# Reordering ScalarE's queue against the weight stream of a two-block fp32 transformer kernel, and reading two last blocks from PSUM

## The chip, the cores and the metric

One Trainium2 chip, one core of it. The metric is the device time of one execution in microseconds (us), as the median of several executions. All data are fp32, batch 1, 256 rows of 2048 channels.

## The reference, cut to what matters

The input `x` passes two blocks. The first has gMLP, dilated and compressed attention, a cross attention and a feed-forward layer of 8192 units. The second, in which nearly all of the change lies, is a gated linear attention over a context and a latent sequence, with an adaptive modulation by a condition, and a SwiGLU:

```python
def second_block(...):
    sh_m, sc_m, gt_m, sh_f, sc_f, gt_f = _modulation(c[:, None, :], w_ada, b_ada)
    csh_m, csc_m, ... = _modulation(c_ctx, w_ada, b_ada)
    h_lat = x * (1.0 + sc_m) + sh_m
    h_ctx = ctx * (1.0 + csc_m) + csh_m
    mix_lat, _ = _token_mixer(h_lat, h_ctx, ...)     # 4 heads, chunks of 64, two directions
    x = _layer_norm(ALPHA * x + gt_m * mix_lat, ln_mix_gain, ln_mix_bias)
    ffn_lat = _swiglu(x * (1.0 + sc_f) + sh_f, w_ffn_in, w_ffn_out)
    return _layer_norm(ALPHA * x + gt_f * ffn_lat, ln_ffn_gain, ln_ffn_bias)
```

`x` here is the first block's output, whose last steps are `x + square(relu(h @ w_up)) @ w_down` and a root mean square norm over the channels.

## The kernel before

**The weight stream.** The kernel is one stream of 974 half slots of weights. SyncE loads 1 MB (two halves, 128x1024 each) into a ring `RW`. For each half ScalarE (ACT) copies it rounded into a ring `RH` (L1161), VectorE (DVE) subtracts that from the weights into `RL` (L1947), and TensorE (PE) multiplies eight 128x128 tiles of both parts into PSUM (L489 the high part against high and low activations, 512 columns; L490 the low part against the high activations, 256 columns; L527 to L529 for products whose activations are the stationary side). `RH` and `RL` hold five halves: before ACT rounds half x it waits until PE has used half x - 4 (`a.wait_ge(s["used"], x - NR + 1)`, with NR = 5). A block is four halves for most products. At a block's end ACT copies the low sum from PSUM to the buffer `LT` (L1166), and DVE adds `LT` and then the high sum from PSUM to what the block is for (L2006, L2279 with L2281, L2825). The modulated input, like every input of a product, is a pair of buffers `AH` (rounded) and `AL` (the rest), drawn as `A` in the views.

**Lanes.** Every engine has its own queue, which it works off in order. The queues are written by generators, called lanes here: `run(a, b, ...)` lets each lane write one step, in the order of its arguments, and again until all are at their end. One such round is a tick; in most of them one half is multiplied. Inside one tick the argument order decides which lane's instructions come first in an engine's queue, and it was one order for all engines. `schedule()` calls the same lanes for each engine. `after(n, lane)` starts a lane n ticks late, `idle(n)` is a lane of n empty ticks, `chain` sets lanes one behind another, `both` side by side.

**The places the change touches**, in the order of the program:

- *last_down with modulate_ctx*: the last column blocks of `w_down`, and beside them the modulation of the context. For a pair of channel tiles DVE scales (L2436), ACT rounds the result into `AH` (L1556), DVE makes the rest `AL` (L2426).
- *scale_x with k2*: the sum of squares of the norm. DVE adds up squares (L2028), PE sums over partitions (L582, L583), ACT makes the reciprocal root (L1235, L1241). The first halves of `w_k` (`k2`) are beside it.
- *context heads*: four heads (`ctx_head`), each with a decay (PE L909), transposes of the weighted keys (PE L950, which need DVE L2562) and the states (PE L929), beside `v2` and `k2`.
- *q2 with modulate_lat*: the modulation of the latent rows, the same lines as above, beside the product with `w_q`.
- *latent heads*: `lat_head(h)` beside `v2` and `bg2`. A direction's queries `Q4` (DVE L2636) are needed by PE L1017. `bg2` makes the merge gates: at each of its blocks' ends DVE adds the sum up in `GB` (L2006), and ACT stores `GB` by a DMA (L1764, to `gate`), for which it waits for DVE.
- *out2*: the block output's product; its evaluation is `gated` (L2825), then the mean and the squares of the layer norm.
- *fin with modulated_ffn*: the first halves of `w_ffn_in`, whose input is modulated in eight pairs of channel tiles: DVE removes the mean (L2834) and scales (L2885), ACT rounds (L1887), DVE makes the rest (L2882); then `x` itself is scaled (DVE L2891, ACT L1894). PE needs pair p at an eighth of the first block pair's halves, in order.
- *fout part 2*: the last product, with `gated` and the final layer norm behind it (ACT's lanes in all this are at L1549, L1655, L1878).

Of the kernel before, what the change touches and what calls it, by code (L numbers as in the profile page):

```python
# [15 lines left out]
S = 256  # L16
# [144 lines left out]
class Lanes:  # L161
    pass
# [986 lines left out]
def scalar_program(nc, m, io):  # L1149
    a, s, l = nc.scalar, m.s, m.l  # L1150
    num, banks, later = Numbers(), Banks(m), Later()
    L = Lanes()

# [9 lines left out]
    def low_part(g):  # L1163

        a.wait_ge(s["used"], num.half)
        a.activation(pair2(m.LT[g % 2]), m.sum_l[g % 2], ACT.Copy).then_inc(s["lt"], 1)  # L1166

    def gemm(blocks, halves, evac, zipped=False):
        rest, g0 = None, num.block
        num.block += blocks  # L1170
        for b, c in steps(blocks, halves, zipped):
            prepare(num.half)
            num.half += 1
            if rest is not None:
                next(rest, None)
            yield
            if c == halves - 1:
                if rest is not None:
                    exhaust(rest)
                low_part(g0 + b)  # L1180
                if num.factor is not None:
                    next(num.factor, None)
                rest = evac(b, g0 + b)
                next(rest, None)
                if b % 2 == 1 and b + 1 < blocks:
                    yield
        exhaust(rest)
        yield
# [570 lines left out]
    def bg2():  # L1759
        def evac(b, g):  # L1760
            n, i = divmod(num.kept, 2)
            num.kept += 1
            a.wait_ge(m.pair[g % 2], g // 2 + 1)
            a.dma_start(io["gate"][n][:, i * 512:i * 512 + 512], m.GB).then_inc(l["kept"], 16)  # L1764
            yield
        yield from gemm(4, 4, evac)
# [106 lines left out]
    def out2():  # L1873
        a.preload_act_table_set("natural_log_exp_and_others")
        yield from gemm(8, 4, normed(0))
        num.last_of_a = num.half
# [39 lines left out]
    def fout(part, first, n):  # L1916
        if part == 2:
            a.preload_act_table_set("natural_log_exp_and_others")
        yield from gemm(8, n // 4, normed(1) if part == 2 else nothing)
        num.fouts.append(num.half)  # L1920
# [15 lines left out]
def vector_program(nc, m, io):  # L1936
# [13 lines left out]
    def gemm(blocks, halves, evac, zipped=False):  # L1950
        rest, g0 = None, num.block
        num.block += blocks
        for b, c in steps(blocks, halves, zipped):
# [5 lines left out]
            if c == halves - 1:  # L1959
                num.lt += 1  # L1960
# [809 lines left out]
    def gated_x(N, which, mods):  # L2770
# [10 lines left out]
        def evac(b, g):  # L2781
# [4 lines left out]
            gated(which, b, g)  # L2786
# [28 lines left out]
    def gated(which, p, g):  # L2815

        v.wait_ge(s["lt"], num.lt)
# [3 lines left out]
        for low in (True, False):  # L2821
            for i in range(2):
                x = m.X[:, (2 * p + i) * S:(2 * p + i + 1) * S]
                part = m.LT[g % 2][:, i * S:i * S + S] if low else m.sum_h[g % 2][:, i, :]
                r = v.scalar_tensor_tensor(x, part, m.mod(which, 2 * p + i), x, ALU.mult, ALU.add)  # L2825
# [25 lines left out]
    L.out2 = lambda: gemm(8, 4, gated_x(0, 2, 20))  # L2851
# [61 lines left out]
    def fout(part, first, n):  # L2913
# [3 lines left out]
        yield from gemm(8, n // 4, evac)  # L2917
# [241 lines left out]
def schedule(L):  # L3159
# [34 lines left out]
    for h in range(4):  # L3194
        run(slow(L.lat_head(h), 1.0 if h == 3 else 1.42), chain(idle() if h == 3 else L.v2(), L.bg2()))
# [10 lines left out]
    run(chain(L.fin(0, 8), L.fin(8, 4), L.fout(0, 0, 16), L.fin(12, 4), L.fin(16, 4), L.fout(1, 16, 16),  # L3206
              L.fin(20, 2), L.fout(2, 32, 12)), modulated, after(10, L.ada((5,), (2.2,))))
# [153 lines left out]
```

## Time and profile before

| | |
|---|---|
| time, 3 runs | 3120.05 us median (3114.98 to 3121.35) |
| the profiled execution's own time | 3117.38 us, its span 3116.0 us |
| PE / DVE / ACT busy | 3004.7 / 2178.2 / 1464.0 us (96%, 70%, 47%) |
| mean granted clock of PE | 0.983 of 2.4 GHz |

The profile is of one execution. "Busy" is time in which an engine works on an instruction; what an engine waited for is inferred from the semaphore that came last. The granted clock is 1.00 at 2.4 GHz and 0.50 at 1.2 GHz.

### The profile page before, as it was taken

Reading aid. Unit: us, or ns where it says so; the run is one execution under the profiler, and the core shown is the slowest. Engines: PE = TensorE matmul, PEld = TensorE weight load, DVE = VectorE, ACT = ScalarE, POOL = GpSimd, SP = SyncE. Lnnn points to the kernel's source line nnn. Section 1 sums busy time; section 2 is a strip of 40 time slices with the busy share of each in tenths; the row PEclk is TensorE's granted clock in tenths of the full one; section 3 lists DMA queues with packets and bytes.
Section 4 is the critical chain, followed back from the end, with each engine's and each line's share of the span. In section 5 each row is a group of like instructions: output and inputs, shape, how many; then the busy total and the mean of one; then the engine's idle time right before and its main releaser. Section 6 shows DMA issues by size and latency. Waiting matters only on the chain.

```text
span 3116.0 us, 40256 instructions
## 1 busy us (share of the span) xinstructions
PE 3004.7 (96%) x16588; PEld 2559.7 (82%) x16588; DVE 2178.2 (70%) x2686; ACT 1464.0 (47%) x1955; POOL 8.5 (0%) x21
## 2 busy tenths in 40 slices
PE   8999898999999999999999999999998999999998
PEld 7887787888888888777787777888877888888886
DVE  6455866899899886677766666648886775555557
ACT  5434654544444444445444443544545444444444
POOL 0000000000000000000000000000000000000000
PEclk9989998999999999999999999999999999999999
DMA  6535233677767785456654444558644775555552
GB/s 257 193 143 180 105 137 122 224 262 259 259 251 267 288 310 203 162 210 246 233 209 163 179 170 173 215 216 330 222 177 182 284 263 185 185 185 189 189 188 109
DMA packets 106661, 648.60 MB, mean 208 GB/s; under 512 B 11856, under 2 KB 11856, under 8 KB 42352
## 3 DMA queue, kind: packets, MB, share of 16 engines
q1 hardware_dynamic: 99936, 621.86, 54.5%
q10 hardware_dynamic: 4608, 16.78, 1.4%
q0 software_dynamic: 1936, 7.41, 0.7%
q8 instruction: 131, 2.15, 0.3%
q14 instruction: 50, 0.41, 0.0%
HBM read 635.52 MB, written 10.49 MB: 207 GB/s over the span
## 4 chain that ended last, share of the span: by engine, by line
PE 78%; DVE 14%; ACT 4%; issue 3%; DMA 0%; SPq 0%; ACTq 0%; DVEq 0%
PE PS L489 41%; PE PS L490 21%; DVE RL L1947 5%; PE PS L527 3%; PE PS L529 3%; PE PS L528 3%; DVE G L2358 2%; ACT RH L1161 2%; PE PS L1017 1%; PE PS L727 1%; PE PS L929 1%; DVE G L2006 1%; ACT G L1362 1%; DVE X L2279 0%; DMA RW<-in_w_ckv 0%
## 5 line engine op out<-in xcount | busy, mean ns | idle before, releaser
L489 PE MATMUL PS<-A,RH 128*128 128x512 f32 x4544 | 1634.5, 404 | 42.1 <-DVE RL L1947 14.9
L1947 DVE TENSOR_TENSOR RL<-RW,RH 128x1024 fp32r<-128x1024 f32 x974 | 1178.3, 1222 | 606.5 <-ACT RH L1161 601.3
L1161 ACT ACTIVATE RH<-RW 128x1024 fp32r<-128x1024 f32 x974 | 1014.0, 1054 | 732.3 <-PE PS L490 585.0
L490 PE MATMUL PS<-A,RL 128*128 128x256 f32 x4544 | 1281.6, 282 | 0.0
L489 PEld LDWEIGHTS PS<-A,RH 128*128 128x128 f32 x4544 | 864.7, 190 | 260.1 <-issue 36.3
L490 PEld LDWEIGHTS PS<-A,RL 128*128 128x128 f32 x4544 | 869.1, 191 | 3.2 <-issue 2.6
L489 PE MATMUL PS<-H,RH 128*128 128x512 f32 x2304 | 816.4, 396 | 5.0 <-DVE RL L1947 5.0
L490 PE MATMUL PS<-H,RL 128*128 128x256 f32 x2304 | 652.0, 283 | 0.0
L489 PEld LDWEIGHTS PS<-H,RH 128*128 128x128 f32 x2304 | 433.4, 188 | 107.2 <-issue 4.0
L490 PEld LDWEIGHTS PS<-H,RL 128*128 128x128 f32 x2304 | 433.9, 188 | 0.4
L1166 ACT ACTIVATE LT<-PS 128x512 f32<-128x512 f32 x234 | 139.2, 595 | 354.9 <-PE PS L490 354.5
L2358 DVE SCALAR_TENSOR_TENSOR G<-G,SILT 128x1024 f32<-128x1024 f32 x210 | 263.5, 1278 | 8.4 <-DMA G<-in_w_ada 8.4
L527 PE MATMUL PS<-RH,A 128*128 128x512 f32 x416 | 166.5, 400 | 0.1
L529 PE MATMUL PS<-RL,A 128*128 128x512 f32 x416 | 162.8, 391 | 0.0
L528 PE MATMUL PS<-RH,A 128*128 128x512 f32 x416 | 162.7, 391 | 0.0
L2006 DVE TENSOR_TENSOR G<-PS,LT 128x512 f32<-128x512 f32 x116 | 79.7, 687 | 87.0 <-ACT LT L1166 80.9
L527 PEld LDWEIGHTS PS<-RH,A 128*128 128x128 f32 x416 | 78.5, 189 | 19.8 <-issue 3.2
L528 PEld LDWEIGHTS PS<-RH,A 128*128 128x128 f32 x416 | 78.4, 189 | 17.1 <-issue 1.4
L529 PEld LDWEIGHTS PS<-RL,A 128*128 128x128 f32 x416 | 78.5, 189 | 16.7
L1525 ACT ACTIVATE G<-G 128x512 f32<-128x512 f32 x32 | 20.2, 632 | 130.8 <-DVE G L2391 130.8
L1362 ACT ACTIVATE G<-G,SM 128x256 f32<-128x256 f32 (+1 forms) x56 | 24.8, 444 | 67.3 <-DVE SM L2175 67.3
L2825 DVE SCALAR_TENSOR_TENSOR X<-LT,MODT,X 128x256 f32<-128x256 f32 x64 | 28.2, 482 | 38.6 <-ACT LT L1166 38.2
(253 smaller groups left out, 1606.9 us busy)
## 6 DMA issues: line engine op xcount, KB each, us to landing
RW<-in_w_fin SPq DMA_DIRECT2D x88, 1024.0 KB, 4.8
G<-in_w_ada SPq DMA_DIRECT2D x160, 512.0 KB, 5.9
RW<-in_w_up SPq DMA_DIRECT2D x64, 1024.0 KB, 5.0
RW<-in_w_down SPq DMA_DIRECT2D x64, 1024.0 KB, 5.0
RW<-in_w_fout SPq DMA_DIRECT2D x44, 1024.0 KB, 4.8
RW<-in_w_v SPq DMA_DIRECT2D x32, 1024.0 KB, 4.8
RW<-in_w_bg SPq DMA_DIRECT2D x32, 1024.0 KB, 5.0
RW<-in_w_k SPq DMA_DIRECT2D x16, 1024.0 KB, 4.8
```

The costliest lines, as they stand in the source:

```text
L489: t.matmul(bank[:, :], wh[:, k, cols], x, start=first and k == 0, stop=False, skip_group_check=True)
L490: done = t.matmul(bank[:, 0:256], wl[:, k, cols], x[:, 0, :], start=False, stop=last and k == 3, skip_group_check=True)
L527: t.matmul(out, xh, wh[:, k, :], start=first and k == 0, stop=False, skip_group_check=True)
L528: t.matmul(out, xl, wh[:, k, :], start=False, stop=False, skip_group_check=True)
L529: done = t.matmul(out, xh, wl[:, k, :], start=False, stop=last and k == 1, skip_group_check=True)
L727: done = t.matmul(bk.ap[:, i * 128:i * 128 + 128], v, pt[0:n, j * 128:j * 128 + 128], start=x == 0, stop=x == len(ops) - 1)
L1161: a.activation(m.high(x), m.slot(j)[:, x % 2 * HC:x % 2 * HC + HC], ACT.Copy).then_inc(s["hi"], 1)
L1166: a.activation(pair2(m.LT[g % 2]), m.sum_l[g % 2], ACT.Copy).then_inc(s["lt"], 1)
L1362: x = a.activation(sc[:, i * n:i * n + n], src[:, i * n:i * n + n], ACT.Exp, bias=sm[:, i:i + 1], scale=scale, accum_out=sm[:, 2 + i:3 + i])
L1947: v.tensor_tensor(m.low(x), m.slot(j)[:, x % 2 * HC:x % 2 * HC + HC], m.high(x).bitcast(F32), ALU.subtract).then_inc(s["lo"], 1)
L2006: v.tensor_tensor(pair2(out), m.sum_h[g % 2], pair2(m.LT[g % 2]), ALU.add).then_inc(m.pair[g % 2], 1)
L2358: v.scalar_tensor_tensor(acc, m.ada_slot[cb][at], silu, acc, ALU.mult, ALU.add).then_inc(s["av"], 1)
```

## The change

On ACT alone (`weights_first`), the products' lane comes before the lane beside it in each tick, in six places; on DVE, PE and SyncE the lane comes first. In last_down and in fin the products came first on every engine before, so what changes there is DVE's order (and nothing in ACT's). The sum of squares (`scale_x`) begins two ticks later. The idle tick between context heads 1 and 2 stands ahead of head 0 instead. The latent modulation takes one step ahead of the first tick. ACT's stores of the gate come two ticks later. And in the last block of `out2` and of the last `fout`, DVE reads the low sum from PSUM itself and ACT's copy is gone (`direct`). No instruction of SyncE or GpSimd moves.

```diff
 class Lanes:
+    weights_first = False
+    def beside(self, lane, products):
+        return (products, lane) if self.weights_first else (lane, products)
...
+    L.weights_first = True          # in ScalarE's lanes only
...
-    def low_part(g):
+    def low_part(g, last=False):
+        if last:
+            return
         a.wait_ge(s["used"], num.half)
         a.activation(pair2(m.LT[g % 2]), m.sum_l[g % 2], ACT.Copy).then_inc(s["lt"], 1)
...
-                low_part(g0 + b)
+                low_part(g0 + b, direct and b == blocks - 1)
...
+        if late:
+            yield
+            exhaust(rest)
+            return
         exhaust(rest)
         yield
...
             num.kept += 1
+            yield
+            yield
             a.wait_ge(m.pair[g % 2], g // 2 + 1)
             a.dma_start(io["gate"][n][:, i * 512:i * 512 + 512], m.GB).then_inc(l["kept"], 16)
             yield
-        yield from gemm(4, 4, evac)
+        yield from gemm(4, 4, evac, late=True)
...
-    def gated(which, p, g):
-
-        v.wait_ge(s["lt"], num.lt)
+    def gated(which, p, g, direct=False):
+
+        if direct:
+            v.wait_ge(s["used"], num.half)
+        else:
+            v.wait_ge(s["lt"], num.lt)
...
-                part = m.LT[g % 2][:, i * S:i * S + S] if low else m.sum_h[g % 2][:, i, :]
+                part = m.sum_h[g % 2][:, i, :]
+                if low:
+                    part = m.sum_l[g % 2][:, i, :] if direct else m.LT[g % 2][:, i * S:i * S + S]
...
-    run(L.last_down(), after(6, L.modulate_ctx()))
-    run(L.scale_x(), L.k2(0, 0, 2))
+    run(*L.beside(after(6, L.modulate_ctx()), L.last_down()))
+    run(*L.beside(after(2, L.scale_x()), L.k2(0, 0, 2)))
     L.low_rank(0)
     beside = L.ada((4,), (2.25,))
-    run(chain(L.ctx_head(0), L.ctx_head(1), idle(1), L.ctx_head(2), L.ctx_head(3)),
-        chain(L.v2(), L.v2(), L.k2(0, 2, 2), L.v2(), L.v2()), beside=beside)
-    run(L.modulate_lat(), L.last_states(), L.q2(), beside=beside)
+    heads = chain(idle(1), L.ctx_head(0), L.ctx_head(1), L.ctx_head(2), L.ctx_head(3))
+    run(*L.beside(heads, chain(L.v2(), L.v2(), L.k2(0, 2, 2), L.v2(), L.v2())), beside=beside)
+    modulated = L.modulate_lat()
+    next(modulated)
+    run(*L.beside(both(modulated, L.last_states()), L.q2()), beside=beside)
...
-        run(slow(L.lat_head(h), 1.0 if h == 3 else 1.42), chain(idle() if h == 3 else L.v2(), L.bg2()))
+        run(*L.beside(slow(L.lat_head(h), 1.0 if h == 3 else 1.42), chain(idle() if h == 3 else L.v2(), L.bg2())))
...
-    run(chain(L.fin(0, 8), L.fin(8, 4), L.fout(0, 0, 16), L.fin(12, 4), L.fin(16, 4), L.fout(1, 16, 16),
-              L.fin(20, 2), L.fout(2, 32, 12)), modulated, after(10, L.ada((5,), (2.2,))))
+    products = chain(L.fin(0, 8), L.fin(8, 4), L.fout(0, 0, 16), L.fin(12, 4), L.fin(16, 4), L.fout(1, 16, 16),
+                     L.fin(20, 2), L.fout(2, 32, 12))
+    run(*L.beside(modulated, products), after(10, L.ada((5,), (2.2,))))
```

The changed file has more lines ahead of these places, so its numbers are higher: L1161 becomes L1169 (rounding), L1166 L1176, L1947 L1963, L2834 L2855, L2885 L2906, L2882 L2903, L489 and L490 L496 and L497, L582 and L583 L589 and L590.

**DVE's queue at the start of fin.** L1947 is the subtraction of one half of weights, L2834, L2885 and L2882 are the modulation. Before:

```order
1612 L2882 SCALAR_TENSOR_TENSOR A<-G,SM,A 128x256 x2
1613 L1947 TENSOR_TENSOR RL<-RW,RH 128x1024
1614 L2834 TENSOR_TENSOR X<-X,RS 128x512
1615 L2885 SCALAR_TENSOR_TENSOR G<-X,SM,RS 128x256 x2
1616 L2882 SCALAR_TENSOR_TENSOR A<-G,SM,A 128x256 x2
1617 L1947 TENSOR_TENSOR RL<-RW,RH 128x1024
```

The same place of the changed kernel:

```order
1602 L2903 SCALAR_TENSOR_TENSOR A<-G,SM,A 128x256 x2
1603 L2855 TENSOR_TENSOR X<-X,RS 128x512
1604 L2906 SCALAR_TENSOR_TENSOR G<-X,SM,RS 128x256 x2
1605 L2903 SCALAR_TENSOR_TENSOR A<-G,SM,A 128x256 x2
1606 L1963 TENSOR_TENSOR RL<-RW,RH 128x1024
1607 L2855 TENSOR_TENSOR X<-X,RS 128x512
```

In each tick the modulation now stands ahead of the subtraction; ACT's queue there is as it was.

**PE's queue at the sum of squares** (L582 and L583, behind the last half of `w_down`, whose input is `H`, and around the first halves of `w_k`, whose input is `A`). Before:

```order
6449 L489 MATMUL PS<-H,RH 128x512
6450 L490 MATMUL PS<-H,RL 128x256
6451 L582 MATMUL PS<-G,C 128x256
6452 L583 MATMUL PS<-G,C 128x256
6453 L489 MATMUL PS<-A,RH 128x512
```

The same two matmuls in the changed kernel:

```order
6481 L496 MATMUL PS<-A,RH 128x512
6482 L497 MATMUL PS<-A,RL 128x256
6483 L589 MATMUL PS<-G,C 128x256
6484 L590 MATMUL PS<-G,C 128x256
6485 L496 MATMUL PS<-A,RH 128x512
```

They stand 32 matmuls, which is two halves, further back.

**ACT's queue in latent head 3**, around a store of the gate (L1764, now L1780) and the roundings beside it. Before:

```order
783 L1617 ACTIVATE G<-G 128x512
784 L1161 ACTIVATE RH<-RW 128x1024
785 L1166 ACTIVATE LT<-PS 128x512
786 L1764 DMA gate<-G 128x512
787 L1161 ACTIVATE RH<-RW 128x1024 x3
```

In the changed kernel:

```order
793 L1631 ACTIVATE G<-G 128x512
794 L1176 ACTIVATE LT<-PS 128x512
795 L1169 ACTIVATE RH<-RW 128x1024 x2
796 L1780 DMA gate<-G 128x512
797 L1169 ACTIVATE RH<-RW 128x1024 x2
```

Two roundings now stand between the copy and the store.

## Rows read from the trace of the kernel before

**Rows 1.** The page: busy time of each engine, and the chain that ended last

```profile
PE 3004.7 (96%) x16588; PEld 2559.7 (82%) x16588; DVE 2178.2 (70%) x2686; ACT 1464.0 (47%) x1955; POOL 8.5 (0%) x21
...
PE 78%; DVE 14%; ACT 4%; issue 3%; DMA 0%; SPq 0%; ACTq 0%; DVEq 0%
```

**Rows 2.** PE's waits over the span: waited for, us, times, longest

```profile
PE PS L489 <- DVE RL L1947: 19.9, 15, 10.9
PE PS L489 <- DVE A L2882: 12.1, 5, 4.5
...
PE PS L489 <- DVE A L2426: 4.8, 3, 2.3
...
PE PS L582 <- DVE G L2028: 4.3, 2, 3.6
PE PS L950 <- DVE G L2562: 3.5, 2, 2.8
...
PE PS L909 <- DVE ALR L2462: 2.1, 2, 1.1
...
PE PS L1017 <- DVE G L2636: 1.4, 1, 1.4
```

**Rows 3.** Windows: stretch, length, busy of PE, PEld, DVE, ACT, POOL; PEclk, DMA share, GB/s

```profile
1224.47:1246.95 22.48, 22.48 (x130) 19.70 (x129) 15.61 (x26) 10.31 (x14) 0.00 (x0) 1.00 0.55 196
1246.95:1264.43 17.48, 15.03 (x82) 12.23 (x81) 14.03 (x20) 10.13 (x13) 0.00 (x0) 1.00 0.50 180
1303.76:1315.64 11.88, 8.27 (x38) 6.89 (x37) 5.28 (x7) 4.12 (x6) 0.00 (x0) 0.86 0.37 142
1362.20:1377.21 15.01, 12.18 (x53) 9.14 (x51) 11.94 (x18) 5.17 (x7) 0.00 (x0) 0.89 0.48 187
1500.69:1519.90 19.21, 14.38 (x66) 11.59 (x65) 14.20 (x20) 6.34 (x9) 0.00 (x0) 0.82 0.47 177
2334.78:2339.34 4.56, 4.56 (x16) 3.90 (x17) 3.39 (x6) 1.85 (x3) 0.00 (x0) 0.59 0.00 0
2339.34:2365.42 26.08, 18.45 (x82) 14.89 (x81) 18.56 (x33) 10.19 (x17) 0.00 (x0) 0.81 0.23 81
2365.42:2397.74 32.32, 29.14 (x161) 24.57 (x161) 17.64 (x27) 19.12 (x30) 0.00 (x0) 0.99 0.66 240
2403.36:2442.19 38.83, 38.83 (x226) 33.97 (x225) 31.42 (x31) 19.19 (x22) 0.00 (x0) 1.00 0.76 281
```

**Rows 4.** DVE's timeline in fin: start, us, line, tile, idle before and releaser

```profile
2342.21 1.23 DVE L1947 TENSOR_TENSOR RL<-RW,RH 128x1024 fp32r<-128x1024 f32 x1 [1.14 <-ACT RH L1161]
2343.35 0.68 DVE L2834 TENSOR_TENSOR X<-X,RS 128x512 f32<-128x512 f32 x1
2344.14 0.88 DVE L2885 SCALAR_TENSOR_TENSOR G<-X,SM,RS 128x256 f32<-128x256 f32 x2
2344.94 0.87 DVE L2882 SCALAR_TENSOR_TENSOR A<-G,SM,A 128x256 fp32r<-128x256 f32 x2
```

**Rows 5.** ACT's timeline in fin, same columns

```profile
2345.06 0.91 ACT L1887 ACTIVATE A<-G,SM 128x256 fp32r<-128x256 f32 x2 [2.88 <-DVE G L2885]
2345.87 1.04 ACT L1161 ACTIVATE RH<-RW 128x1024 fp32r<-128x1024 f32 x1
```

**Rows 6.** ACT's timeline in latent head 3

```profile
1895.80 2.01 ACT L1161 ACTIVATE RH<-RW 128x1024 fp32r<-128x1024 f32 x2 [4.51 <-DVE G L2006]
```

**Rows 7.** Timeline of DVE and PE in latent head 0, second direction

```profile
1679.19 0.69 DVE L2636 TENSOR_TENSOR G<-G,SM 128x512 f32<-128x512 f32 x1
...
1679.93 0.70 PE L1017 MATMUL PS<-G 128*128 128x512 f32 x1
```

**Rows 8.** ACT's timeline behind the last weight product

```profile
3096.98 0.60 ACT L1166 ACTIVATE LT<-PS 128x512 f32<-128x512 f32 x1 [4.55 <-PE PS L490]
```

**Rows 9.** One line's instructions: duration in ns, min/median/max

```profile
L2825 DVE SCALAR_TENSOR_TENSOR X<-LT,MODT,X x64: 475/480/489, 2240.2 to 3098.0; 128x256 f32<-128x256 f32 x64
L2825 DVE SCALAR_TENSOR_TENSOR X<-PS,MODT,X x64: 473/480/486, 2241.1 to 3098.9; 128x256 f32<-128x256 f32 x64
```

More of the change, by code:

```diff
@@ L161 @@
 class Lanes:
-    pass
+    weights_first = False
+    def beside(self, lane, products):
+        return (products, lane) if self.weights_first else (lane, products)
 class Later:
@@ L1161, in prepare, with gemm @@
             a.activation(m.high(x), m.slot(j)[:, x % 2 * HC:x % 2 * HC + HC], ACT.Copy).then_inc(s["hi"], 1)
-    def low_part(g):
+    def low_part(g, last=False):
+        if last:
+            return
         a.wait_ge(s["used"], num.half)
         a.activation(pair2(m.LT[g % 2]), m.sum_l[g % 2], ACT.Copy).then_inc(s["lt"], 1)
-    def gemm(blocks, halves, evac, zipped=False):
+    def gemm(blocks, halves, evac, zipped=False, direct=False, late=False):
         rest, g0 = None, num.block
@@ L1874, in out2 @@
         a.preload_act_table_set("natural_log_exp_and_others")
-        yield from gemm(8, 4, normed(0))
+        yield from gemm(8, 4, normed(0), direct=True)
         num.last_of_a = num.half
@@ L1918, in fout @@
             a.preload_act_table_set("natural_log_exp_and_others")
-        yield from gemm(8, n // 4, normed(1) if part == 2 else nothing)
+        yield from gemm(8, n // 4, normed(1) if part == 2 else nothing, direct=part == 2)
         num.fouts.append(num.half)
@@ L1948, in prepare, with gemm @@
                             ALU.subtract).then_inc(s["lo"], 1)
-    def gemm(blocks, halves, evac, zipped=False):
+    def gemm(blocks, halves, evac, zipped=False, direct=False):
         rest, g0 = None, num.block
@@ L1959, in gemm @@
             if c == halves - 1:
-                num.lt += 1
+                num.lt += not (direct and b == blocks - 1)
                 if rest is not None:
@@ L2785, in evac @@
                     v.wait_ge(s["xa"], 4)
-            gated(which, b, g)
+            gated(which, b, g, b == 7)
             evacuated(g)
@@ L2849, in finish @@
         v.wait_ge(s["nrs_a"], 3 * N + 3)
-    L.out2 = lambda: gemm(8, 4, gated_x(0, 2, 20))
+    L.out2 = lambda: gemm(8, 4, gated_x(0, 2, 20), direct=True)
     def gains():
@@ L2916, in fout @@
         evac = gated_x(1, 5, 32) if part == 2 else gated_part
-        yield from gemm(8, n // 4, evac)
+        yield from gemm(8, n // 4, evac, direct=part == 2)
     def gated_part(b, g):
```

## The prediction, made before the changed kernel ran

> **What bounds the kernel now.** I read the page first: PE is busy 3004.7 of 3116.0 us, and the chain that ended last runs through PE for 78%, DVE 14% and ACT 4% [rows 1]. The change removes no matmul, so it can only fill PE's pauses. PE's waits, grouped by what ended them, say which pauses those are: for `RL`, for the modulated pairs (L2882, L2426), for the sum of squares (L2028), for keys of a context head (L2562) and for `Q4` (L2636), 46 us in all with waits that this change doesn't reach (the start of the kernel alone holds 10.9 of `RL`'s 19.9) [rows 2]. The waits leave out what a pause does to the clock, so I priced places by windows that begin and end with a half of weights: an undisturbed half takes 22.48/8 = 2.81 us in `down` and 38.83/14 = 2.77 us in `fin`, both at clock 1.00, while stretches with long pauses show 0.81 to 0.86 and the first half of fin 0.59, which is 4.56 us for 2.77 us of work [rows 3].
>
> **The ring of waits.** In fin a tick takes 4.74 us in a steady pattern. DVE sat idle 1.14 us before its subtraction, waiting for ACT's rounding, and ACT sat idle 2.88 us before its L1887, waiting for DVE's L2885 [rows 4, 5]. DVE can't start the modulation of a tick before that tick's subtraction; ACT can't round before it has done L1887 of the pair before. So neither works ahead, though there are free slots in the ring. With the modulation first on DVE, L2885 no longer stands behind the subtraction that waits for ACT, and the ring is open.
>
> **Part by part**, against the profiled time of 3117.4 us.
>
> *last_down, with the modulation of the context.* Five halves take 17.48 us where 5 x 2.81 = 14.05 are work [rows 3]. The pattern is the one of the ring, with L2436 and L1556. Nothing else limits the stretch: DVE is busy 14.03 of 17.48 us and 15.61 of 22.48 ahead of it. **-3.4**; with the modulation first, the subtraction is late by 2.2 us at most (0.73 + 1.48 us for its pieces at their largest), and the ring holds five halves.
>
> *Sum of squares.* Two halves take 11.88 us, 6.26 above 5.62 [rows 3]. PE's wait is 3.6 us of it [rows 2], the rest the two matmuls of the sum and a slow clock of 0.86. After, PE has two halves (5.5 us) to do first, so L2028 is there in time; the matmuls themselves stay, about 0.5. **-5.8**. Behind it, ACT makes the reciprocal root later by two halves; the scaled `x` isn't read before the latent modulation (`alpha_x` follows q2), which hides it.
>
> *Context heads.* Head 0 starts one tick later. The decay's wait of 1.1 us (L909) goes. The transposes' wait of 2.8 us [rows 2], in a stretch of 15.01 us at clock 0.89 with DVE busy 11.94 [rows 3], goes only in small part: DVE reaches L2562 through work of its own, which moves back by the same tick. With 0.7 us for the smaller wait at head 1 (3.5 less 2.8) **-1.8**, between 0 and -4.5 (all of these waits).
>
> *q2 with the modulation of the latent rows.* Four halves take 19.21 us, 7.97 above 4 x 2.81, at clock 0.82 [rows 3]; 4.8 are PE's waits for L2426 [rows 2]. Here DVE already had the modulation first, and the ring is ACT's: its L1556 waits for DVE, and its rounding stands behind that. One step ahead brings every pair forward by a tick (19.21/4 = 4.8 us), and three ticks lose DVE's idle of 1.1 us before the subtraction, taken from fin's pattern [rows 4]: 8.1 us in all, against 7.97 by which PE would want the last pair earlier. That is just enough: **-7.9**, down to -4 if one pair is late and the clock falls once.
>
> *Latent heads.* Head 3 alone has a wait, 1.4 us for L2636 [rows 2]. ACT stood 4.51 us before its rounding because the store of the gate waits for DVE's L2006 [rows 6], and the subtraction ahead of L2636 waited for that rounding. With the store two ticks later the rounding is early. **-1.4**, by the wait itself, without a slow stretch behind it. A store that lands late could hold DVE's next sum in `GB`: sums are four halves (11.2 us) apart, and two ticks of them (5.6 us) now pass before the store starts. The rows don't show how long it may take; I take no loss, and 1 us for each of the 16 blocks of `bg2` in a rival.
>
> *Last blocks from PSUM.* ACT's copy of 0.60 us goes, at the end of the kernel [rows 8] and at the end of out2, where PE has no weights to multiply meanwhile: **-1.2**. L2825 itself takes 480 ns from `LT` and 480 ns from PSUM [rows 9], so nothing is lost. The Trainium skill's page "VectorE: DVE Perf Modes", in the section "The TRN2 errata — SBUF-src ops pay a fixed extra latency per instruction", has a source in PSUM cost more fixed cycles (120 against 58) than one in SBUF, some 65 ns per instruction at its clock. By it, two reads at each end would give back 0.26 us in all, and the part would bring 0.9. The two rows of this trace do not show the difference, in 64 instructions each (where one operand, `X`, is in SBUF either way).
>
> *fin.* From the first half to the last late one are 4.56 + 26.08 + 32.32 us for 16 halves, which need 16 x 2.77 = 44.4: 18.6 above [rows 3]. The first 1.8 (slow clock behind the layer norm's tail) stay. In the middle 26.08 - 5 x 2.77 = 12.2: after the change a tick of DVE is its own work, from the starts of the rows 1.14 + 0.79 + 0.80 and 0.87 for L2882, 3.6 us in place of 4.74 [rows 4]. The L2882 shown is pair 3's and ends at 2345.8; two idles and one subtraction ahead of it go, 1.14 us each, so it ends at 2342.4, and the next pairs 3.6 us apart: 2346.0, 2349.6, 2353.2. PE multiplies two pairs in a half, but repeats them for the second block before it takes 4: from 2339.34 on it wants pair 3 after 1.5 halves (2343.5), 4 after 3 (2347.7), 5 after 3.5 (2349.0) and 6 half a half later, after its wait for 5 (2351.0). So PE still waits 0.6 and 2.2 us, with one slow half (1.8, as in fin's first) behind. 12.2 - 4.6 is 7.6, and pair 7's early coming (its step is a short one) adds 0.4: 8.0 go. In the last part 32.32 - 27.7 = 4.6 is the ring with L1894 and L2891 in it; 4.0 go. **-12.0**, between -8 and -14.
>
> The sum is 3.4 + 5.8 + 1.8 + 7.9 + 1.4 + 1.2 + 12.0 = **33.5 us**, so 3083.9 for the profiled execution. Its 3117.4 stand 2.7 below the median of the three runs; the median of the changed kernel then is 3120.05 - 33.5 = 3086.55, **3086.5**.
>
> **The rivals.**
>
> *A. As summed*, 3077 to 3096: **0.72**. For it speaks that every term is a stretch with pauses in one place, whose cause is an order that is gone. Its bounds are 0 and -4.5 in the context, -4 in q2, -8 and -14 in fin: between -33.5 + 1.8 + 3.9 + 4.0 = -23.8 (3096.3) and -33.5 - 2.7 - 2.0 = -38.2 (3081.9); the lowest run of before lies 5.1 under its median, and with that the lower end is 3077.
>
> *B. DVE is the limit where the ring was.* In the window of q2 it is busy 14.20 of 19.21 us, in fin's 18.56 of 26.08 [rows 3]; the subtractions that ACT now offers earlier fill its gaps ahead of the modulation. If the pairs come half as early as placed, fin and q2 give 10 instead of 20: **3096.5**, chance **0.14**. Against it: the changed queue puts the modulation first on DVE.
>
> *C. The rounding first costs the heads.* ACT does what it has for a head one rounding (1.04 us [rows 5]) later, and at eight directions and four context heads PE wants the result just when it is there: L2636 ended at 1679.88, PE's L1017 began at 1679.93 [rows 7], and heads 1 and 2 look the same. If each of the 12 is late by 1.04 us, 12.5 us go back, **3099**, chance **0.07**. Against it: rounding first lets DVE's subtraction, which stands in the same queue ahead of the head's pieces, start at once, which is 1 us to the good.
>
> *D, the slower side: a whole tick is lost per head.* If ACT's rounding in its turn waits for PE (the ring is full, slot x - 4 in use), the head's piece behind it waits up to 2.8 us more, and the clock falls as in fin's first half, 1.8. Then 12 x 4.6 = 55 go back against the 33.5: 3120.05 - 33.5 + 55 = **3141.5**; with 7.3 of the 12 places late it is even with before. ACT is busy 47% [rows 1] and mostly waits for PE at its roundings, which speaks for it; the steps of a head that have an idle tick ahead speak against. Chance **0.04**.
>
> *E. The change doesn't do what it says:* pauses reappear as waits for a landing DMA or another semaphore (16 us at the gate stores, the rest where a pair or a key is late again), within 6 us of before, 3114 to 3126: **0.03**.
>
> **How the numbers follow.** About 0.2% (6 us) is what a measurement of this kernel can tell from no change. A, B and C are faster by more, 0.93; D gives slower 0.04; E gives same 0.03. The range is to hold 8 in 10: A's from 3077 on, and it takes in the times of B (3096.5) and C (3099), up to 3100; what is left out is D, E and the tails.
>
> **What would show it.** The granted clock near 1.00 where it was 0.86 and 0.82 (sum of squares, q2). PE's waits for L2028 (but the 0.7 that lie elsewhere) and L2426 gone; those for L2882 down from 12.1 us to some 7, 4.5 of which are the start. DVE's waits for the rounding gone from fin's first twelve halves, and DVE's ticks there 3.6 us. ACT's idle of 4.51 before a rounding gone. The span's end some 0.6 us nearer to the last L490. It is wrong if PE shows new waits of over 1 us at L1017, L950 or L994 (C, D), if DVE's subtraction is late at L489 in places that were quiet, or if DVE waits at L2006 for a store of the gate.

## The result

The changed kernel takes **3080.6 us** (median of 4 runs, 3074.7 to 3082.5) against 3117.5 us of the kernel before beside it (3113.5 to 3121.4): a ratio of 0.9878, 95% interval 0.9858 to 0.9898. Repeated later with five runs it was 3078.2 against 3119.2, 0.9874 (0.9855 to 0.9892). 3086.5 was predicted, 3077 to 3100 as the range. In the profiled executions the span fell from 3116.0 to 3079.4 us, by 36.6; the prediction's sum was 33.5.

The page of the changed kernel, busy time by engine and the chain that ended last:

```profile
PE 2993.7 (97%) x16588; PEld 2553.5 (83%) x16588; DVE 2178.0 (71%) x2686; ACT 1461.0 (47%) x1953; POOL 8.5 (0%) x21
...
PE 85%; DVE 10%; ACT 3%; issue 2%; DMA 1%; SPq 0%; ACTq 0%; DVEq 0%
```

The work is the same (ACT has the two copies less), DVE's share of the chain went from 14% to 10% [rows 1]. PE's waits in the changed kernel:

```profile
PE PS L496 <- DVE RL L1963: 12.5, 4, 11.0
...
PE PS L496 <- DVE A L2903: 6.7, 3, 4.5
...
PE PS L957 <- DVE G L2578: 3.0, 1, 3.0
...
PE PS L916 <- DVE ALR L2478: 1.1, 1, 1.1
...
PE PS L496 <- DVE A L2442: 0.5, 1, 0.5
```

Against [rows 2], `RL` went from 19.9 to 12.5 us (11.0 of it the first load), the pairs of fin from 12.1 to 6.7 (4.5 of it the start), those of q2 from 4.8 to 0.5; the wait for `Q4` and the 3.6 us for the sum of squares are gone. What stands is the context's head 0, 3.0 us. The windows that answer to [rows 3], with the same halves in them (last_down, the sum of squares, the two halves behind it, head 0, q2, then three of fin and fin undisturbed):

```profile
1247.73:1261.77 14.04, 14.04 (x82) 12.30 (x81) 11.86 (x14) 7.56 (x10) 0.00 (x0) 1.00 0.49 177
1301.09:1306.71 5.62, 5.62 (x34) 4.90 (x33) 2.60 (x3) 2.10 (x3) 0.00 (x0) 1.00 0.48 182
1306.71:1313.18 6.47, 6.47 (x38) 5.66 (x37) 4.44 (x5) 3.92 (x6) 0.00 (x0) 1.00 0.50 203
1352.98:1366.97 13.99, 11.01 (x46) 8.64 (x45) 13.42 (x24) 5.18 (x8) 0.00 (x0) 0.88 0.52 201
1491.71:1502.81 11.10, 11.10 (x66) 9.71 (x65) 9.15 (x12) 5.92 (x7) 0.00 (x0) 1.00 0.78 291
2308.98:2313.23 4.25, 4.16 (x16) 3.63 (x17) 4.14 (x10) 2.76 (x5) 0.00 (x0) 0.64 0.00 0
2313.23:2330.02 16.79, 14.61 (x82) 12.22 (x81) 16.19 (x30) 8.82 (x14) 0.00 (x0) 1.00 0.35 126
2330.02:2358.29 28.27, 28.27 (x162) 24.52 (x161) 22.29 (x32) 21.10 (x33) 0.00 (x0) 1.00 0.70 258
2363.94:2403.52 39.58, 39.58 (x226) 34.34 (x225) 28.80 (x28) 17.89 (x20) 0.00 (x0) 1.00 0.75 279
```

last_down takes 14.04 us in place of 17.48, all of it matmuls. The sum of squares took 11.88 and with the next two halves 17.4; now it is 5.62 + 6.47 = 12.1. q2's four halves take 11.10 in place of 19.21. fin's middle takes 16.79 in place of 26.08, its last part 28.27 in place of 32.32.

In fin, DVE's and ACT's timeline of the changed kernel (start, length, line):

```profile
2316.44 1.22 DVE L1963 TENSOR_TENSOR RL<-RW,RH 128x1024 fp32r<-128x1024 f32 x1
2317.58 0.68 DVE L2855 TENSOR_TENSOR X<-X,RS 128x512 f32<-128x512 f32 x1
2318.37 0.88 DVE L2906 SCALAR_TENSOR_TENSOR G<-X,SM,RS 128x256 f32<-128x256 f32 x2
2319.16 0.87 DVE L2903 SCALAR_TENSOR_TENSOR A<-G,SM,A 128x256 fp32r<-128x256 f32 x2
2319.96 1.22 DVE L1963 TENSOR_TENSOR RL<-RW,RH 128x1024 fp32r<-128x1024 f32 x1
```

```profile
2319.28 0.91 ACT L1903 ACTIVATE A<-G,SM 128x256 fp32r<-128x256 f32 x2 [1.65 <-DVE G L2906]
```

DVE's rows stand one behind another without an idle bracket: a tick is 2319.96 - 2316.44 = 3.52 us where it was 4.74 [rows 4], and ACT's idle time before L1903 fell from 2.88 to 1.65 [rows 5]. That DVE is now what sets the pace there is seen from the missing brackets.

### The profile page after: what moved, and what is told of

Its sections match the earlier page's. It is cut to its first block, busy times and chain, and to the rows that moved or that the text cites. A ratio compares the mean times of both kernels' runs of the same rounds, so it can differ in the third digit from the quotient of the medians.

```text
span 3079.4 us, 40253 instructions
## 1 busy us (share of the span) xinstructions
PE 2993.7 (97%) x16588; PEld 2553.5 (83%) x16588; DVE 2178.0 (71%) x2686; ACT 1461.0 (47%) x1953; POOL 8.5 (0%) x21
## 4 chain that ended last, share of the span: by engine, by line
PE 85%; DVE 10%; ACT 3%; issue 2%; DMA 1%; SPq 0%; ACTq 0%; DVEq 0%
PE PS L496 46%; PE PS L497 23%; DVE RL L1963 3%; PE PS L534 3%; PE PS L536 3%; PE PS L535 3%; DVE G L2374 1%; ACT RH L1169 1%; PE PS L734 1%; PE PS L1024 1%; PE PS L936 1%; ACT G L1376 1%; PE PS L870 0%; PE PS L916 0%; DMA RW<-in_w_ckv 0%
## 5 line engine op out<-in xcount | busy, mean ns | idle before, releaser
L496 PE MATMUL PS<-A,RH 128*128 128x512 f32 x4544 | 1629.5, 403 | 28.5 <-DVE RL L1963 11.2
L1963 DVE TENSOR_TENSOR RL<-RW,RH 128x1024 fp32r<-128x1024 f32 x974 | 1178.4, 1222 | 559.3 <-ACT RH L1169 553.0
L1169 ACT ACTIVATE RH<-RW 128x1024 fp32r<-128x1024 f32 x974 | 1015.9, 1054 | 780.9 <-PE PS L497 634.9
L497 PE MATMUL PS<-A,RL 128*128 128x256 f32 x4544 | 1279.4, 282 | 0.0
L496 PEld LDWEIGHTS PS<-A,RH 128*128 128x128 f32 x4544 | 861.7, 190 | 245.5 <-issue 31.6
L497 PEld LDWEIGHTS PS<-A,RL 128*128 128x128 f32 x4544 | 865.6, 190 | 3.1 <-issue 2.6
L496 PE MATMUL PS<-H,RH 128*128 128x512 f32 x2304 | 814.0, 395 | 1.3 <-DVE RL L1963 1.3
L497 PE MATMUL PS<-H,RL 128*128 128x256 f32 x2304 | 651.4, 283 | 0.0
L496 PEld LDWEIGHTS PS<-H,RH 128*128 128x128 f32 x2304 | 432.8, 188 | 101.3 <-issue 1.2
L497 PEld LDWEIGHTS PS<-H,RL 128*128 128x128 f32 x2304 | 433.2, 188 | 0.4
L1176 ACT ACTIVATE LT<-PS 128x512 f32<-128x512 f32 x232 | 138.3, 596 | 346.3 <-PE PS L497 345.9
L734 PE MATMUL PS<-G 128*128 128x128 f32 (+1 forms) x184 | 35.8, 342 | 20.4 <-ACT G L1388 20.4
```

The costliest lines, as they stand in the source:

```text
L496: t.matmul(bank[:, :], wh[:, k, cols], x, start=first and k == 0, stop=False, skip_group_check=True)
L497: done = t.matmul(bank[:, 0:256], wl[:, k, cols], x[:, 0, :], start=False, stop=last and k == 3, skip_group_check=True)
L734: done = t.matmul(bk.ap[:, i * 128:i * 128 + 128], v, pt[0:n, j * 128:j * 128 + 128], start=x == 0, stop=x == len(ops) - 1)
L1169: a.activation(m.high(x), m.slot(j)[:, x % 2 * HC:x % 2 * HC + HC], ACT.Copy).then_inc(s["hi"], 1)
L1963: v.tensor_tensor(m.low(x), m.slot(j)[:, x % 2 * HC:x % 2 * HC + HC], m.high(x).bitcast(F32), ALU.subtract).then_inc(s["lo"], 1)
```

## The experiments

Each is the changed kernel with one or a few edits. Since the places lie far apart, each edit was read in its own window, which is far sharper than the whole time: the halves between the places take the same time from run to run, but for what the last section tells of.

**1. DVE's order of before** in last_down and fin; the other queues untouched.

```diff
-    run(*L.beside(after(6, L.modulate_ctx()), L.last_down()))
+    run(L.last_down(), after(6, L.modulate_ctx()))
...
-    run(*L.beside(modulated, products), after(10, L.ada((5,), (2.2,))))
+    run(products, modulated, after(10, L.ada((5,), (2.2,))))
```

> The changed kernel with VectorE's order of before in last_down and in fin (the subtraction ahead of the modulation); the queues of ScalarE, TensorE and SyncE are those of the changed kernel. Theory of the ring (each of the two engines waits for the other once per tick): the five halves 382 to 386 take 17.5 us again instead of 14.05, the 16 halves 710 to 725 take 62 to 63 us instead of 49.3, a tick of DVE in fin 4.7 us; together 17 us slower, some 3097.5. Rival, that these stretches gained by something else (VectorE's share of work, the clock after the layer norm's tail): under 5 us of it come back.

Measured: 3097.4 us (ratio to before 0.9942, 0.9926 to 0.9959). Windows of last_down and of fin's second and third part:

```profile
1247.78:1265.27 17.49, 15.04 (x82) 12.25 (x81) 14.05 (x21) 10.13 (x13) 0.00 (x0) 1.00 0.49 174
2318.46:2342.99 24.53, 16.62 (x80) 13.54 (x80) 18.30 (x33) 10.20 (x17) 0.00 (x0) 0.92 0.25 86
2342.99:2375.26 32.27, 29.14 (x164) 24.68 (x162) 17.27 (x26) 18.73 (x30) 0.00 (x0) 1.00 0.66 235
```

17.49 us again, and 24.53 + 32.27 = 56.8 against 45.1: 3.4 and 11.7 us come back. A tick of DVE in fin is 4.74 us again (its subtractions start at 2330.47 and 2335.21). This one swap on one engine gives back 15.1 of the 36.6 us by which the span fell.

**2. The same order on both engines**, the lane ahead of the products, in last_down and fin. DVE keeps the new order, ACT gets the other.

```diff
-    run(*L.beside(after(6, L.modulate_ctx()), L.last_down()))
+    run(after(6, L.modulate_ctx()), L.last_down())
...
-    run(*L.beside(modulated, products), after(10, L.ada((5,), (2.2,))))
+    run(modulated, products, after(10, L.ada((5,), (2.2,))))
```

> The changed kernel with the lane ahead of the products on ScalarE too, in last_down and fin: VectorE has the new order and ScalarE the one that it had in q2 before. Theory: what opens the ring is that the two engines have opposite orders; with the same order on both the ring is closed again whichever it is: a tick of fin takes 4.8 us, the 16 halves 710 to 725 some 62 us, last_down's five 17 us: +16 us, 3097. Rival: VectorE's order alone was the fault: the time stays at 3081.

Measured: 3096.5 us, one run. DVE's timeline in fin, and the windows of last_down (halves 381 to 385, which are the late ones here) and of fin's second part:

```profile
2324.63 1.23 DVE L1963 TENSOR_TENSOR RL<-RW,RH 128x1024 fp32r<-128x1024 f32 x1 [1.14 <-ACT RH L1169]
...
2329.37 1.23 DVE L1963 TENSOR_TENSOR RL<-RW,RH 128x1024 fp32r<-128x1024 f32 x1 [1.13 <-ACT RH L1169]
```

```profile
1244.92:1261.80 16.88, 14.77 (x82) 12.25 (x81) 13.13 (x20) 9.27 (x13) 0.00 (x0) 1.00 0.47 173
2319.63:2341.70 22.07, 16.54 (x81) 13.69 (x80) 16.90 (x29) 8.86 (x16) 0.00 (x0) 0.83 0.26 96
```

A tick of fin is 4.74 us, to the hundredth that of the kernel before, with the same idle 1.14 us. In last_down DVE's idle before the subtraction is back too, 1.05 us in each of two ticks. So the fault was neither engine's order by itself but that both had the same one. The windows give back a little less than in experiment 1: 16.88 us of the 17 expected (2.8 of the 3.4), and 22.07 + 32.82 = 54.9 in fin against 45.1 (9.8 of the 13.3; with the half ahead of them 60.2, where 62 were expected). Halves 712 and 713 of fin, slow in experiment 1 (4.42 and 3.33 us), take 2.82 and 2.83 here; that fits the lane first, which puts each pair ahead of its tick's subtraction, but wasn't tried apart.

**3. ACT's lane first** at the sum of squares, in the context and latent heads, and in q2; the step ahead and the late store stay.

```diff
-    run(*L.beside(both(modulated, L.last_states()), L.q2()), beside=beside)
+    run(both(modulated, L.last_states()), L.q2(), beside=beside)
```

and the same at the three other places.

> The changed kernel with ScalarE's lane ahead of its rounding, as before, at the sum of squares, the context heads, q2 and the latent heads; the step ahead in q2, the late gate store and everything else stay. Theory: the rounding first matters in q2 alone, where three ticks get VectorE's idle of 1.05 us before the subtraction back: about 3 us slower, 3083 to 3084; sum of squares, context and latent heads within 0.5 us. Rival C of the prediction, that rounding first costs the heads 1.04 us at up to 12 places: then this kernel is faster than the changed one there, by up to 12 us. Third: the whole gain of q2 and head 3 is the rounding's: 9 us slower.

Measured: 3086.2 us (0.9900, 0.9885 to 0.9915). q2's four halves:

```profile
1492.37:1509.57 17.20, 13.19 (x67) 11.00 (x66) 12.50 (x17) 7.44 (x10) 0.00 (x0) 0.90 0.59 213
```

17.20 us, where the changed kernel has 11.10 and the one before 19.21: with the rounding second, 6.1 us come back in q2, twice the 3 that were expected, and nothing at the latent heads' store, which the third expectation had counted in. What the other 2.0 us are is seen in experiment 4. The sum of squares takes the same time to 0.01 us, the context heads together to 0.2, the latent heads together to 0.4 (0.3 of it at halves 570 and 571). So the order of ACT costs nothing in the heads and brings next to nothing, and rival C and D have no ground. `Q4` even comes earlier than before; DVE's L2652 and PE's L1024 in the changed kernel, at the place of [rows 7]:

```profile
1658.94 0.69 DVE L2652 TENSOR_TENSOR G<-G,SM 128x512 f32<-128x512 f32 x1
...
1660.26 1.02 PE L1024 MATMUL PS<-G 128*128 128x512 f32 x2
```

It is there at 1659.6, more than half a microsecond ahead of 1660.2, where it was 0.05.

**4. q2 and the latent heads as before** (no step ahead, ACT's lane first, the gate stored at once).

```diff
-            yield
-            yield
             a.wait_ge(m.pair[g % 2], g // 2 + 1)
...
-    modulated = L.modulate_lat()
-    next(modulated)
-    run(*L.beside(both(modulated, L.last_states()), L.q2()), beside=beside)
+    run(L.modulate_lat(), L.last_states(), L.q2(), beside=beside)
```

> The changed kernel with q2 (no step ahead, ScalarE's lane first) and the latent heads (lane first, store of the gate at once) as before the change. Theory: head 3 waits again 1.4 us for Q4, 1.9 us with what follows; the ends of blocks at 509, 533, 557 0.2 us each; q2's halves 452 to 457 7 to 8 us. Together +10, 3090. Rival, that part of q2's gain stems from the context heads ahead of it (which now end earlier against VectorE's modulation): under 5 us come back there.

Measured: 3091.2 us, one run. PE's wait for `Q4`, and ACT's rounding behind the store:

```profile
PE PS L1024 <- DVE G L2650: 1.4, 1, 1.4
```

```profile
1882.01 2.01 ACT L1169 ACTIVATE RH<-RW 128x1024 fp32r<-128x1024 f32 x2 [4.51 <-DVE G L2020]
```

Both are back to the value of before [rows 2, 6]. Over all latent heads 2.4 us come back, 1.7 of them in this one half and 0.2 at three block ends; experiment 3, with the late store and the lane first, had 0.3 of it. So the gain in the latent heads is the store's, but for those 0.3. In q2 the four halves, and the last of the four by itself, take here, and the last in experiment 3 takes:

```profile
1489.17:1506.88 17.71, 11.90 (x66) 9.71 (x66) 13.78 (x20) 6.73 (x9) 0.00 (x0) 1.00 0.54 200
1503.98:1506.84 2.86, 2.86 (x17) 2.53 (x18) 2.60 (x3) 0.87 (x1) 0.00 (x0) 1.00 0.00 0
```

```profile
1505.48:1509.90 4.42, 4.42 (x16) 3.80 (x17) 4.17 (x4) 1.82 (x2) 0.00 (x0) 0.62 0.02 6
```

That is 6.6 us more than the changed kernel, not 8.1, though q2's queues are those of before. The difference comes with the clock of the last half: it took 4.79 us in the profile of before, 2.86 here at clock 1.00, and 4.42 in experiment 3 at clock 0.62. So the step ahead is not the 2.0 us that experiment 3 alone suggests. Half by half, it is worth 1.7 us at q2's first half (4.51 us here against 2.77 in experiment 3). The rounding first is worth 4.5 us at the third half (7.24 us in experiment 3 against 2.77 in the changed kernel), and behind that pause stands a half that is slow by 1.6 us or more in some profiles and not in others. Two mixtures were not tried, because by the queues' order the engines would wait for one another for good: the rounding first with the gate stored at once, and the rounding first in q2 without the step ahead. The late store and the step ahead are thus also what lets ACT round first.

**5. Three starts and ends undone**: the sum of squares at once, the idle tick between heads 1 and 2, the two last blocks through `LT`.

```diff
-    run(*L.beside(after(2, L.scale_x()), L.k2(0, 0, 2)))
+    run(*L.beside(L.scale_x(), L.k2(0, 0, 2)))
...
-    heads = chain(idle(1), L.ctx_head(0), L.ctx_head(1), L.ctx_head(2), L.ctx_head(3))
+    heads = chain(L.ctx_head(0), L.ctx_head(1), idle(1), L.ctx_head(2), L.ctx_head(3))
```

and `direct` taken as false throughout.

> The changed kernel with three edits undone, far apart in the program: the sum of squares starts at once (no two ticks), the idle tick stands between context heads 1 and 2 again, and the two last blocks go through ScalarE's copy and LT. Theory, each read in its own window: halves 401 to 404 take 6.26 - 0.93 = 5.3 us more; halves 411 to 431 of the context 1.9 us more, of which 1.2 at the decay; the end of out2 and the end of the kernel 0.6 us each. Together +8.4, 3089. Rival for PSUM: reading it costs VectorE 0.13 us at each end by the cycles a page gives, so only 0.5 each come back. Rival for the sum of squares: ScalarE's order alone hides it, nothing comes back.

Measured: 3085.0 us, one run. PE's waits there:

```profile
PE PS L957 <- DVE G L2579: 4.3, 2, 2.9
PE PS L589 <- DVE G L2045: 3.6, 1, 3.6
PE PS L916 <- DVE ALR L2479: 2.1, 2, 1.1
```

Halves 401 to 404 take 5.4 us more: 6.3 at the pause, less 0.9 that the two matmuls of the sum cost between the halves of `w_k` in the changed kernel. The context takes 2.7 us more, where 1.9 were expected: 1.2 at the decay and 1.6 in front of head 1's transposes. The end of the kernel takes 0.63 us more, out2's pause before its L1101 as well. That reading PSUM costs DVE nothing is seen in the changed kernel's last block, where four reads from PSUM follow the last weight matmul at once:

```profile
3061.05 1.79 DVE L2846 SCALAR_TENSOR_TENSOR X<-PS,MODT,X 128x256 f32<-128x256 f32 x4 [3.83 <-PE PS L497]
3062.87 0.69 DVE L2795 TENSOR_TENSOR X<-X,RS 128x512 f32<-128x512 f32 x1
```

They take 1.82 us from start to the next line's start, the two from `LT` and two from PSUM of before 1.83. The 0.13 us at each end, an estimate from the cycles in the Trainium skill's page "VectorE: DVE Perf Modes" (its section "The TRN2 errata — SBUF-src ops pay a fixed extra latency per instruction"), aren't there; the measurement decides.

**6. Two more steps ahead in fin, one tick of delay for the sum of squares.**

```diff
     modulated = L.modulated_ffn()
     next(modulated)
+    next(modulated)
+    next(modulated)
...
-    run(*L.beside(after(2, L.scale_x()), L.k2(0, 0, 2)))
+    run(*L.beside(after(1, L.scale_x()), L.k2(0, 0, 2)))
```

> The changed kernel with fin's modulation two more steps ahead of the first tick on every engine (so two subtractions of VectorE, which have some 20 us to spare there, come behind them), and the sum of squares one tick late in place of two. If VectorE's own work is what is left of fin's wait, pair 6 comes 2.3 us earlier: PE's waits of 0.23 and 1.95 us in halves 714 and 715 go to nothing or 0.2 and half 714 takes 3 us instead of 5.4. If it is ScalarE's part, they stay. Sum of squares: half 402 is followed by a wait of some 0.8 to 1.0 us (L2028's result was 3.6 us late with no tick between, one half is 2.8), halves 401 to 404 take 1 us more than the changed kernel's; with two ticks it was all hidden.

Measured: 3076.3 us, one run. PE's waits and fin's second part:

```profile
PE PS L496 <- DVE A L2903: 4.8, 1, 4.8
...
PE PS L589 <- DVE G L2044: 1.4, 2, 0.8
```

```profile
2313.78:2327.91 14.13, 14.13 (x80) 12.19 (x79) 13.53 (x27) 7.54 (x13) 0.00 (x0) 0.98 0.40 148
```

The waits for pairs 5 and 6 are gone, 14.13 us in place of 16.79 (of which the clock of the half ahead takes a part, see experiment 9): what was left in fin was DVE's own work, in the way of pairs that were wanted sooner. The sum of squares has a wait of 0.8 us with one half to hide it; two are needed.

**7. Two steps ahead in q2.**

```diff
     modulated = L.modulate_lat()
     next(modulated)
+    next(modulated)
```

> The changed kernel with the latent modulation two steps ahead of q2's first tick instead of one. In q2 PE waits 0.54 us for its first pair alone, which is behind a piece that waits for its weights' DMA, and that doesn't change. So nothing by the theory, within 0.3 us in halves 451 to 457; if the pairs were still short in supply, the wait at the first pair grows by 1.4 us (a step's work) and none goes.

Measured: 3075.5 us, one run; halves 451 to 457 take 0.35 us more than in the first profile of the changed kernel, at the first pair, and none of the others changes. The repeated profile of the changed kernel (experiment 9) takes 0.24 more there as well, so the second step does nothing that can be told from chance. The whole time is within the spread of the changed kernel's runs.

**8. The weights' products (`ada`) 12 ticks later** beside the context heads.

```diff
-    beside = L.ada((4,), (2.25,))
+    beside = after(12, L.ada((4,), (2.25,)))
```

> The changed kernel with the products for the modulation's weights (VectorE L2374, 1.28 us apiece, on weights that a DMA brings) begun 12 ticks later beside the context heads. If head 0's keys are late because VectorE is full there, PE's wait of 2.98 us at L957 falls by about the pieces that stand ahead of L2578 in that head, two or three of them: to 0 to 0.5 us, with 1.5 us of slow halves behind it, -4 us in halves 419 to 423. If ScalarE or a DMA is what is late, the wait stays. The piece that waited 1.17 us for its weights ahead of q2 stands elsewhere too: q2's first pair is then 1.2 us earlier and PE's 0.54 us there go. The heads behind may wait more.

Measured: 3077.0 us, one run. The windows of head 0, of q2, and of three halves of `w_v` behind it:

```profile
1347.71:1358.13 10.42, 9.42 (x46) 7.49 (x45) 9.63 (x20) 5.18 (x8) 0.00 (x0) 1.00 0.45 184
1481.74:1494.54 12.80, 11.39 (x66) 9.73 (x65) 10.60 (x16) 5.80 (x7) 0.00 (x0) 1.00 0.86 328
1580.29:1594.60 14.31, 11.67 (x50) 9.30 (x49) 9.12 (x11) 3.18 (x3) 0.00 (x0) 0.88 0.54 211
```

Head 0 takes 10.42 in place of 13.99 us and its wait falls from 3.0 to 1.0, so DVE's load is what made it late. From halves 403 to 451 5.0 us are gained, but q2 takes 1.7 more than its 11.10, and the halves of `w_v`, where the lane now has its end, 6 us more than 8.2. Together it is a loss of 3 to 4 us; that the one run is quick is chance ahead of the change (5.3 us in halves 0 to 381, whose queues are those of the changed kernel) and a shorter undisturbed half behind half 716 (the last section).

**9. Timed beside one another, five rounds:** the changed kernel, the changed kernel with fin's two steps, and that with `ada` 12 ticks later and denser.

```diff
     modulated = L.modulated_ffn()
     next(modulated)
+    next(modulated)
+    next(modulated)
```

```diff
-    beside = L.ada((4,), (2.25,))
+    beside = after(12, L.ada((4,), (1.85,)))
```

> The changed kernel again, as it is, for the two beside it and for the size of the gain: 3081 within 3 us, by the sum of the places that were read (3.4, 5.3, 1 to 3, 7.2, 2.3, 1.2, 13). TensorE's period of an undisturbed half in five stretches (halves 153 to 193, 228 to 257, 458 to 468, 573 to 613, 716 to 783) is again either 2.77 or 2.83 us, and not the same in each stretch as in the first profile; if the change had set it, it would be.

> The changed kernel with fin's modulation two more steps ahead. By the first look at this edit half 714 loses 2.6 us and with it all of PE's waits there; 2.5 us faster than the changed kernel beside it, 3078.5. Rival, that the time is given back behind it (ring drained at half 716, where the first look left 1.3 us of room): the same as the changed kernel.

> z1 with the weights' products for the modulation begun 12 ticks later and written 1.85 ticks apart in place of 2.25, so that they end about where they ended. The start 12 ticks later took 5.0 us off the context heads and gave 2.5 us back in q2 and 7 us in w_k and w_v behind it, where the lane was still unfinished. If its lateness cost those 7, they go now and 2 to 3 us are left beside z1, 3076. If VectorE's work as a whole is what counts from the heads to q2, the denser pieces make the heads and q2 wait and nothing is left, 3078 to 3080.

Measured: 3078.2 (ratio to before 0.9874, 0.9855 to 0.9892), 3079.5 (four runs; 0.9875, 0.9859 to 0.9890) and 3089.6 us (0.9911, 0.9896 to 0.9927). The two steps don't show in the whole: the kernel with them isn't faster than the changed one. Its profile has, for fin's second part and the two halves behind it:

```profile
2315.24:2329.38 14.14, 14.14 (x82) 12.22 (x81) 13.54 (x27) 7.58 (x13) 0.00 (x0) 1.00 0.42 148
2329.38:2335.78 6.40, 6.09 (x35) 5.01 (x33) 6.40 (x11) 6.25 (x10) 0.00 (x0) 1.00 0.45 166
```

Against the first profile of the changed kernel 2.65 us are gained and 0.7 given back (6.40 for two halves of 2.83), since the deferred subtractions are now late at half 716. But the second profile of the changed kernel has, for fin's first half and its second part:

```profile
2314.85:2320.11 5.26, 5.26 (x16) 4.50 (x17) 5.16 (x11) 2.77 (x5) 0.00 (x0) 0.50 0.00 0
2320.11:2335.91 15.80, 14.43 (x82) 12.31 (x82) 15.20 (x29) 9.14 (x14) 0.00 (x0) 1.00 0.36 134
```

Here the first half took 5.26 us at clock 0.50, where it was 4.25 at 0.64, and the second part 15.80 in place of 16.79: where DVE sets the pace, what PE loses in one half it waits less in a later one. Over the 16 halves 710 to 725 the two profiles agree, 49.31 and 49.32 us, and the kernel with the two steps takes 47.88. The 1.4 us left are under what five rounds tell. The denser `ada` is slower by 10 us: the pieces fill DVE where heads 2 and 3 and q2 need it (halves 440 and 450 take 3.4 and 4.0 us more, q2's four 14.8 in place of 11.1).

## Why the prediction was right, step by step

Windows before against after, with what an experiment gave back when it undid the place:

| place | predicted | measured | undone |
|---|---|---|---|
| last_down | -3.4 | -3.4 | +3.4 (1) |
| sum of squares | -5.8 | -5.3 | +5.4 (5) |
| context heads | -1.8 | -1.8 | +2.7 (5) |
| q2, halves 451 to 457 | -7.9 | -7.3 | +6.5 (4) |
| latent heads | -1.4 | -2.6 | +2.4 (4) |
| two last blocks | -1.2 | -1.3 | +1.3 (5) |
| fin, halves 711 to 725 | -12.0 | -13.3 | +11.7 (1) |

In fin the undone version lacks 1.6 us of the 13.3. Its middle ran at clock 0.92 where the one before shows 0.81, with PE busy for 16.62 and 18.45 us [rows 3]; the low clock fell beside the window, on halves 726 and 727, which took 7.20 us there and 5.62 before. The column of the measured adds to 35.0; the other 1.6 of the 36.6 us lie where no queue was changed (below, the last section), so they are not the change's: its places gave 35.0 us where 33.5 were forecast.

*The ring* was the right cause: in fin and last_down experiments 1 and 2 show it from both sides, in q2 experiment 3 from ACT's. DVE's tick in fin was forecast at 3.6 us and is 3.52.

*fin* was under-sized by 1.3. The waits came as worked out, for pairs 5 and 6 with 0.2 and 1.9 us (0.6 and 2.2), but the slow half of 1.8 us that was charged behind them did not come: the clock in that window is 1.00. It is 1.00 in the second profile as well.

*Sum of squares*: the two matmuls were put at 0.5 us and cost 0.9 between two halves.

*q2*: the size held, the working did not, so that its nearness is in part luck. It said that one step ahead brings every pair forward by a tick, 4.8 us, and the idle of DVE 3.2. The tick was mis-sized: 4.8 is the window divided by four, while DVE's subtractions in the kernel before stand 3.52 us apart there:

```profile
1504.26 1.22 DVE L1947 TENSOR_TENSOR RL<-RW,RH 128x1024 fp32r<-128x1024 f32 x1 [1.05 <-ACT RH L1161]
...
1507.78 1.22 DVE L1947 TENSOR_TENSOR RL<-RW,RH 128x1024 fp32r<-128x1024 f32 x1 [1.05 <-ACT RH L1161]
```

And the two parts have their weights the other way round: experiments 3 and 4 give 1.7 us to the step ahead and 4.5 to the rounding first, and up to 2 us of the 8.1 hang on whether the last half runs at a low clock. And 1.1 us were given back at a place the prediction did not have: half 451 took 7.31 us and takes 8.41, because the heads end earlier and DVE stands before a piece whose weights are not there, in front of the first pair of q2:

```profile
1479.16 1.28 DVE L2374 SCALAR_TENSOR_TENSOR G<-G,SILT 128x1024 f32<-128x1024 f32 x1 [1.17 <-DMA G<-in_w_ada]
1480.36 1.38 DVE L2452 TENSOR_SCALAR G<-X,MODT 128x256 f32<-128x256 f32 x4
```

In experiment 8, where that lane is 12 ticks later, DVE has no idle ahead of the piece that stands there (1467.41) and half 451 takes 7.30 us, as before. That fits; but the heads are quicker there too, so no run shows the DMA as the cause with all else equal.

*Latent heads*: the store was the cause, as put; the term left out what stands behind the wait in the same half (1.7 us with it) and three block ends of 0.2 us.

*Context heads*: the sum held. Undoing the idle tick alone gave 2.7 back, not 1.8, since with rounding first head 1's transposes wait 0.7 us more without that tick than they did before; why was not tried.

*The rivals.* B (DVE as the limit) is true of fin's middle, where it was already in the term, and of what is left: experiments 6, 8 and 9 move it about. C and D fell with experiment 3. E's DMA wait exists, at 1.1 us. A store of the gate that holds DVE up is not to be seen.

## What to carry to other kernels

Where two engines hand work to each other in both directions, look at the order in each one's queue: in fin, last_down and q2 the same order on both closed a ring that cost each of them a wait per tick, and opposite orders opened it with no work removed. At the sum of squares and in the heads the order made no difference of note (experiment 3), so look first for the idle time on both engines in the same tick. Price such places by windows from one undisturbed step to another, since the waits leave out slow clock and small delays; and where a stream is sped up, look at once for what is timed by something else beside it, here the weights of another lane. A gain of 2 us in a window may be real and still not be worth an edit if the program's own spread is 8.

## What the runs showed of the hardware

In many stretches an undisturbed half of weights has two durations, and which it is changes from one execution to the next in the same place. Halves 583 to 612, 30 halves of the same instructions (first of the kernel before, then the changed kernel, then the changed kernel again):

```profile
1943.74:2028.54 84.80, 84.80 (x482) 73.50 (x481) 50.85 (x52) 44.52 (x53) 0.00 (x0) 1.00 0.57 209
```

```profile
1921.50:2004.70 83.20, 83.20 (x482) 72.78 (x481) 50.81 (x52) 44.31 (x53) 0.00 (x0) 1.00 0.59 213
```

```profile
1925.41:2010.21 84.80, 84.80 (x482) 73.58 (x481) 50.84 (x55) 44.52 (x53) 0.00 (x0) 1.00 0.58 210
```

2.827 or 2.773 us per half, at clock 1.00 in all, with nothing between in the 13 profiles; such a pitch holds over a whole stretch and can be another behind an interruption (in experiment 4 it is 2.77 up to half 468 and 2.83 from half 471 on, with halves of 5.03 and 4.45 us between). Ahead of the sum of squares, in `w_down`, it is 2.81 in every profile. In the stretch up to half 783 the first profile of the changed kernel has the longer and that of before the shorter, which from half 726 to 782 is 3.0 us against the change; around q2 and behind it it is the other way. With it go halves that in some executions run at a low clock and in others do not, in places where the queues are the same (half 470: 4.46 us at clock 0.62 in the profile before, 2.88 at 1.00 after; half 683: 4.56 and 3.00). These, and 10 us of spread among all profiles in halves 0 to 381, are why the whole times of one kernel differ by 8 to 13 us and why a window says more than they do. What sets the pitch was not found.
